# Splitting more of the input projections into upper and lower parts, and moving GpSimd's long steps behind the state space's preparation

## What is computed

```python
z = x @ w_in[i]
u_pool, q, k, v, u_ssm = jnp.split(z, splits, axis=-1)      # 256, 384, 384, 384, 384 columns
y_pool = pool_mixer(u_pool, w_pool[i], pool_scale[i])       # trailing means over 2, 4, 8, 16 tokens
y_attn = chunk_attention(q, k, v, rel_bias[i])              # chunks of 64, own and 8 before
y_ssm = s5_mixer(u_ssm, ...)                                # complex diagonal state space, scan over tokens
heads = jnp.concatenate([rms_norm(y_pool), rms_norm(y_attn), rms_norm(y_ssm)], axis=-1)
h = layer_norm(DN_ALPHA * x + heads @ w_out[i])
x = layer_norm(DN_ALPHA * h + moe(h) + sigmoid(h @ w_ple_gate[i]) * (p[i] @ w_ple_proj[i]))
```

## Time and profile before

| | |
|---|---|
| median of 3 runs | 456.39 us (455.49 to 456.59) |
| the profiled execution's own time | 456.71 us |
| its span | 454.9 us |
| busy: PE, DVE, ACT, POOL | 97%, 74%, 49%, 26% |
| mean granted TensorE clock | 0.993 |

### The profile page before, as it was taken

How to read it: one execution, slowest core, us unless ns; L and a number is a source line. 1 busy time by engine, 2 the same in 40 slices (tenths; PEclk the granted TensorE clock), 3 DMA queues, 4 the chain that set the end, 5 groups by cost and what they waited for, 6 DMA issues and landing times.

```text
span 454.9 us, 5417 instructions
## 1 busy us (share of the span) xinstructions
PE 439.2 (97%) x1933; PEld 297.3 (65%) x1933; DVE 335.7 (74%) x515; ACT 223.5 (49%) x367; POOL 116.2 (26%) x146
## 2 busy tenths in 40 slices
PE   8999999999999999999999999999999999999992
PEld 4444664487676556677687767777777777777651
DVE  3699969885536989998484165778878776789677
ACT  3110461051987850215101155788887777789522
POOL 7880042470056500000007410122212222111200
PEclk9999999999999999999999999999999999999997
DMA  8995023235992981111930239999999999840583
GB/s 273 382 377 161 0 41 87 46 99 152 409 385 72 316 305 46 48 46 55 398 149 2 34 108 424 406 423 418 415 394 369 365 368 371 328 204 20 210 224 139
DMA packets 37049, 103.15 MB, mean 227 GB/s; under 512 B 16028, under 2 KB 22092, under 8 KB 30240
## 3 DMA queue, kind: packets, MB, share of 16 engines
q1 hardware_dynamic: 27728, 91.68, 53.2%
q0 software_dynamic: 5600, 9.44, 6.6%
q10 hardware_dynamic: 3696, 1.71, 1.4%
HBM read 95.39 MB, written 17.86 MB: 249 GB/s over the span
## 4 chain that ended last, share of the span: by engine, by line
PE 70%; DVE 12%; DMA 11%; ACT 4%; issue 1%; SPq 1%; DVEq 0%
PE bank L1298 8%; PE bank L1114 6%; PE bank L946 6%; PE bank L1125 5%; PE bank L1270 5%; DMA region_b<-in_w_exp_down 4%; PE bank L1275 4%; PE bank L1279 4%; PE bank L1283 4%; PE bank L1197 3%; PE bank L1199 3%; PE bank L1198 3%; PE bank L1211 3%; DMA region_b<-in_ssm_par 3%; PE bank L1254 2%; DMA region_b<-expert_scratch 2%
## 5 line engine op out<-in xcount | busy, mean ns | idle before, releaser
L946 PE MATMUL bank<-region_e,region_a 128*128 128x512 f32 x128 | 56.0, 596 | 0.0
L946 PEld LDWEIGHTS bank<-region_e,region_a 128*128 128x128 f32 x128 | 24.0, 190 | 29.7 <-issue 28.7
L1275 PE MATMUL bank<-gate_up_upper,tokens_upper 128*128 128x512 f32 x96 | 36.3, 459 | 0.0
L1114 PE MATMUL bank<-region_b,region_e 128*128 128x512 f32 x68 | 32.9, 607 | 0.0
L568 POOL DMA_INDIRECT slot_scratch<-region_h,slot_i x8 | 8.4, 1054 | 87.2 <-issue 87.2
L581 POOL DMA_INDIRECT expert_scratch<-region_g,region_h x8 | 10.0, 1256 | 80.0 <-ACT region_g L892 80.0
L1823 DVE TENSOR_TENSOR gate_up_lower<-region_a,gate_up_upper 128x1024 fp32r<-128x1024 f32 x24 | 28.0, 1221 | 3.3 <-ACT gate_up_upper L865 3.3
L1279 PE MATMUL bank<-gate_up_upper,tokens_lower 128*128 128x512 f32 x96 | 29.8, 392 | 0.0
L1197 PE MATMUL bank<-ple_gate_upper,hidden_upper 128*128 128x512 f32 x64 | 26.6, 415 | 0.0
L865 ACT ACTIVATE gate_up_upper<-region_a 128x1024 fp32r<-128x1024 f32 x24 | 23.7, 1056 | 3.2 <-DMA region_a<-in_w_exp_down 3.2
L1199 PE MATMUL bank<-ple_gate_upper,hidden_lower 128*128 128x512 f32 x64 | 25.0, 391 | 0.0
(11 more groups left out here) (346 smaller groups left out, 1073.1 us busy)
## 6 DMA issues: line engine op xcount, KB each, us to landing
region_a<-in_w_exp_gate SPq DMA_DIRECT2D x8, 1024.0 KB, 8.1
region_a<-in_w_exp_up SPq DMA_DIRECT2D x8, 1024.0 KB, 17.9
region_a<-in_w_exp_down SPq DMA_DIRECT2D x8, 1024.0 KB, 17.7
region_a<-in_w_in SPq DMA_DIRECT2D x3, 1536.0 KB, 16.6
region_b<-in_w_out SPq DMA_DIRECT2D x1, 4096.0 KB, 14.6
expert_scratch<-zero_scratch SPq DMA_DIRECT2D x8, 512.0 KB, 10.1
region_b<-in_w_exp_gate SPq DMA_DIRECT2D x4, 1024.0 KB, 10.1
region_b<-in_w_exp_up SPq DMA_DIRECT2D x4, 1024.0 KB, 17.6
```

The lines of the kernel that those rows point to most:

```text
L946: last = mm(bank[bank_i][:], w[:, k, m * P:(m + 1) * P], xT[:, k, :], start=(k == 0), stop=(k == KD - 1))
L1114: last = mm(bank[WO_AT[half][group]][:], hdT[:, k, t * P:(t + 1) * P], w_o[:, k, half * 512:half * 512 + 512], start=(i == 0), stop=(i == ...
L1275: mm(out_, x_hi[r][:, k * P:(k + 1) * P], w_hi[:, k], start=False, stop=False)
```

## The change

Six of the eight slices of the state input, all three query tiles and the first key tile are multiplied in upper and lower parts. ACT makes the upper parts (`ux_hi`, `uw_hi` in three pairs of slices, `qw_hi`, `kw_hi`), DVE the lower ones (`u_lower(0..2)`, `qw_lo`, `kw_lo`), into areas that other tensors use later. The loads come in five pairs instead of four, `w_q` stands ahead of `par`. All three query tiles now stand ahead of the first scores, the first pool tile behind the turns, and the last key tile ahead of the second scores. POOL zeroes `m0` after the first key tile (`pe_qk` 4), since `ux_hi` uses its space, and does the doublings of m = 8, 16 and 32 once `cp` and the kernel's inputs are ready (`kern_in` 4). The zero copy of SP waits for that zeroing. DVE normalises heads 0 and 1 behind the scan instead of ahead of the rotation.

```diff
-FIRST_K = (0, 1, 2, 4, KD)
-QK_ORDER = (("q", 0), ("k", 0), ("q", 1), ("q", 2), ("k", 1), ("k", 2))
+FIRST_K = (0, 1, 2, 4, 6, KD)
+QK_ORDER = (("q", 0), ("q", 1), ("q", 2), ("k", 0), ("k", 1), ("k", 2))
@@ sync
+            load(w_q, w_in_v[:, :, POOL_W:POOL_W + ATT_W], "wq_in")
             load(par[:, C_BRE:SSM_COLS], io["ssm_par"][:, C_BRE:SSM_COLS], "par_in")
-            load(w_q, w_in_v[:, :, POOL_W:POOL_W + ATT_W], "wqk_in")
...
-            sp.wait_ge(S["const_set"], 1)
+            sp.wait_ge(S["rot_ready"], 2)
             sp.dma_start(zero_d, RH[:, 3072:3072 + D]).then_inc(S["ye_zero"], 16)
@@ gpsimd
-            link(g.memset(m0, 0.0))
...
             while m < NC:
+                if m == 8:
+                    gp.wait_ge(S["rb_in"], 16)
+                    g.memset(rbias[0:64, :, 192:256], NEG).then_inc(S["rot_ready"], 1)
+                    gp.wait_ge(S["pe_qk"], 4)
+                    g.memset(m0, 0.0).then_inc(S["rot_ready"], 1)
+                    gp.wait_ge(S["kern_in"], 4)
@@ scalar, behind the sines
+            for i in range(3):
+                ac.wait_ge(S[f"x_in{2 + i}"], 32)
+                k = slice(2 + 2 * i, 4 + 2 * i)
+                a.activation(ux_hi[...], xT[:, k, :], ACT.Copy).then_inc(S["xw_hi_set"], 1)
+                a.activation(uw_hi[...], w_ssm[:, k, :], ACT.Copy).then_inc(S["xw_hi_set"], 1)
+            ac.wait_ge(S["wq_in"], 16)
+            a.activation(qw_hi[...], w_q[:, 2:KD, :], ACT.Copy).then_inc(S["xw_hi_set"], 1)
@@ scalar, behind the copies of the state tiles
+            ac.wait_ge(S["wqk_in"], 16)
+            a.activation(kw_hi[...], w_k[:, 2:KD, 0:P], ACT.Copy).then_inc(S["xw_hi_set"], 1)
@@ tensor
+            def u_term(i, w, x, stop=False):
+                for m in range(3):
+                    for k in (2 * i, 2 * i + 1):
+                        last = mm(bank[m][:], w[:, k * SSM_W + m * P:...], x[:, k * T:(k + 1) * T],
+                                  start=False, stop=(stop and k == 5))
+            for i in range(3):
+                pe.wait_ge(S["xw_hi_set"], 2 * i + 2)
+                u_term(i, uw_hi, ux_hi)
+                pe.wait_ge(S["xw_lo_set"], 2 * i + 1)
+                u_term(i, uw_hi, ux_lo)
+                pe.wait_ge(S["xw_lo_set"], 2 * i + 2)
+                u_term(i, uw_lo, ux_hi, i == 2)
+            def qk_split(n, w, w_hi, w_lo, width, parts):
...
+                pe.wait_ge(S["xw_hi_set"], parts)
+                for x in (ux_hi, ux_lo):
...
+                pe.wait_ge(S["xw_lo_set"], parts)
...
-            qk(0)
-            qk(1)
-            project(POOL_BANKS[0], w_up, 0, "pe_pool")
+            for n in range(3):
+                qk_split(n, w_q, qw_hi, qw_lo, ATT_W, 7)
+            pe.wait_ge(S["wqk_in"], 16)
+            qk_split(3, w_k, kw_hi, kw_lo, P, 8)
...
-            pe.wait_ge(S["qk_done"], 2)
+            pe.wait_ge(S["qk_done"], 4)
             scores(0)
@@ vector
+            def u_lower(i):
+                dv.wait_ge(S["xw_hi_set"], 2 * i + 1)
+                tt(ux_lo[...], xT[:, k, :], ux_hi[...], ALU.subtract).then_inc(S["xw_lo_set"], 1)
+                dv.wait_ge(S["xw_hi_set"], 2 * i + 2)
+                tt(uw_lo[...], w_ssm[:, k, :], uw_hi[...], ALU.subtract).then_inc(S["xw_lo_set"], 1)
...
             cmul(bb[:, 0], bb[:, 1], b_re, b_im, ...)
+            dv.wait_ge(S["xw_hi_set"], 7)
+            tt(qw_lo[...], w_q[:, 2:KD, :], qw_hi[...], ALU.subtract).then_inc(S["xw_lo_set"], 1)
...
-            normalise(0)
-            normalise(1)
             dv.wait_ge(S["pe_x"], 1)
-            dv.wait_ge(S["rot_ready"], 1)
+            dv.wait_ge(S["rot_ready"], 3)
...
+            normalise(0)
+            normalise(1)
             add_bias(2)
```

More of the change, by code:

```diff
@@ L246, in trunk @@
         hd_lo = {k: over(f"heads_lower{k}", T - P, R0 + 4 * (k * T + P)) for k in WO_SPLIT}
+        ux_hi = over("input_upper", 6 * T, H0 + 4 * 3072)
+        uw_hi = over("state_weights_upper", 6 * SSM_W, C0)
+        ux_lo = over("input_lower", 6 * T, C0 + 4 * 3072)
+        qw_hi = over("query_weights_upper", 6 * ATT_W, G0 + 4 * 1536)
+        qw_lo = over("query_weights_lower", 6 * ATT_W, A0 + 4 * (O_Q + 2 * ATT_W))
+        kw_hi = over("key_weights_upper", 6 * P, H0 + 4 * 6144)
+        kw_lo = over("key_weights_lower", 6 * ATT_W, A0 + 4 * (O_K + 2 * ATT_W))
+        uw_lo = over("state_weights_lower", 6 * SSM_W, A0 + 4 * 2 * SSM_W)
         bank = [ctx.enter_context(nc.psum_tensor(f"bank{i}", [P, 512], F32)) for i in range(8)]
@@ L320, in _ @@
             xv = io["xT"].rearrange("(p k) t -> p k t", k=KD)
-            for i in range(4):
+            for i in range(5):
                 ks = slice(FIRST_K[i], FIRST_K[i + 1])
@@ L508, in _ @@
             link(g.tensor_copy(dec, mag8[:].unsqueeze(2).broadcast_to([P, Q, NC])))
[L509 to L512, removed]
+            g.memset(dec[:, :, 0:1], 0.0).then_inc(S["rot_ready"], 1)
+            gp.wait_ge(S["rot_ready"], 3)
             gp.wait_ge(S["gp_in"], 16 * 4)
@@ L683, in _ @@
             qk_copy(1)
+            qk_copy(2)
             ac.wait_ge(S["bx_ready"], 2)
@@ L951, in _ @@
                 mm(bank[7][:, 0:P], ones[:], ones[:], start=True, stop=True)
-            for k in range(KD):
-                if k in FIRST_K:
-                    pe.wait_ge(S[f"x_in{FIRST_K.index(k)}"], 32)
+            for k in range(2):
+                pe.wait_ge(S[f"x_in{k}"], 32)
                 for m in range(3):
-                    last = mm(bank[m][:], w_ssm[:, k, m * P:(m + 1) * P], xT[:, k, :], start=(k == 0), stop=(k == KD - 1))
-                    if k == KD - 1:
-                        last.then_inc(S["pe_u"], 1)
+                    mm(bank[m][:], w_ssm[:, k, m * P:(m + 1) * P], xT[:, k, :], start=(k == 0), stop=False)
+            def u_term(i, w, x, stop=False):
+                for m in range(3):
+                    for k in (2 * i, 2 * i + 1):
+                        last = mm(bank[m][:], w[:, k * SSM_W + m * P:k * SSM_W + (m + 1) * P], x[:, k * T:(k + 1) * T],
+                                  start=False, stop=(stop and k == 5))
+                    if stop:
+                        last.then_inc(S["pe_u"], 1)
+            for i in range(3):
[5 more added lines that the diff above has]
+                u_term(i, uw_lo, ux_hi, i == 2)
             def qk(n):
@@ L962, in qk @@
                 project(QK_BANKS[n], w_q if name == "q" else w_k, m, "pe_qk")
+            def qk_split(n, w, w_hi, w_lo, width, parts):
+                _, m = QK_ORDER[n]
+                dst = bank[QK_BANKS[n]][:]
+                for k in range(2):
+                    mm(dst, w[:, k, m * P:(m + 1) * P], xT[:, k, :], start=(k == 0), stop=False)
+                pe.wait_ge(S["xw_hi_set"], parts)
+                for x in (ux_hi, ux_lo):
+                    for k in range(6):
+                        mm(dst, w_hi[:, k * width + m * P:k * width + (m + 1) * P], x[:, k * T:(k + 1) * T], start=False, stop=False)
+                pe.wait_ge(S["xw_lo_set"], parts)
+                for k in range(6):
+                    last = mm(dst, w_lo[:, k * ATT_W + m * P:k * ATT_W + (m + 1) * P], ux_hi[:, k * T:(k + 1) * T], start=False, stop=(k == 5))
+                last.then_inc(S["pe_qk"], 1)
             def v_tile(t, bank_i):
```

53 lines of the change are left out of this document (35 added, 18 removed).

## The result

The changed kernel takes 466.76 us in the median of 6 runs (465.59 to 467.53), the kernel before 456.14 (455.35 to 456.59): the ratio is 1.023 [1.021, 1.025]. It is slower by 2.3%, outside the range of the prediction, whose forecast was 0.2% faster. The profiled execution took 465.68 us, 9.0 more than that of before.

What follows compares the result with a forecast made beforehand. TensorE was taken as full, VectorE as almost as long, with Y held by the moved states. Y starting 0.9 us earlier gave 456.7 - 0.9 = 455.8, on the runs' scale 455.5 us; range 453.7 to 458.3.

Steps and rivals of the forecast that it cites:

- What bounds the kernel, and that the moved states decide Y's start: TensorE full, VectorE almost as long; the moved states release the Y stage at 93.6 instead of 94.5, 0.9 us earlier.
- TensorE's saving: 42 split matmuls take 7.8 us off TensorE, which stands at Y at 89.5, 5.0 us earlier than before.
- The idle time at the third slice: TensorE waits for ScalarE's rounding after slices 0 and 1: 2.4 us idle until 12.8, against 0.45 before.
- ssm_par 4.1 us later, 22.2: Load queued behind the query weights; VectorE's complex product starts at 22.2, 4.1 us later.
- The lower parts, the steps without GpSimd beside them: VectorE: lower parts add 2.6 and 1.0 us, steps without GpSimd give near 6.9 back; cp ends at 56.9.
- The zeroing beside cp costs nothing: GpSimd's zeroing of m0 at 49 to 52 beside VectorE's 3072-column products: 0 taken, bounds 0 and 2.7 us.
- GpSimd's 13.0 us now on the path: GpSimd's late doublings and decay copy behind cp take 13.0 us and release the rotation at 70.0.
- The wait ahead of Y: TensorE, ready early, waits about 4 us ahead of the Y stage for the moved states.
- The fall in it: Clock falls from 2.4 to 1.2 GHz some 2.2 us after TensorE stops, read from the kernel's end.
- The forecast's own sum: Profiled time 456.7 less 0.9 us for Y's earlier start gives 455.8, or 455.5 on the runs' scale.
- the first rival: Clock falls in the wait ahead of Y, costing 1.6 to 1.8 us of Y: 457.2; chance 0.26.
- The bound from the row: Upper bound of the clock rival's loss: 10.8 us if all of Y ran at half rate.

Runs made afterwards that it cites:

- the fill: Changed kernel plus five thrown-away 384-column matmuls on TensorE ahead of its wait for the Y stage: 455.03 us, ratio 0.997.
- the doubling: Changed kernel with GpSimd's last doubling (32 columns a group) moved to VectorE: four executions at 452.8 to 454.6 us, two at 461.8 and 462.1.
- both: Changed kernel with the last doubling on VectorE and two thrown-away matmuls ahead of the wait for Y: 453.13 us, ratio 0.994.
- the fourth term: Changed kernel with a lower-by-lower term added to each of its 42 split products: 461.88 us, ratio 1.012.
- three additions: Kernel before plus three thrown-away VectorE additions of 1536 columns ahead of the last step of the scanned states: 474.18 us, ratio 1.039.
- two additions: Kernel before plus two thrown-away VectorE additions of 1536 columns ahead of the last step of the scanned states: 470.99 us, ratio 1.031.
- dense work behind the wait: Changed kernel plus eight thrown-away 384-column matmuls on TensorE behind the wait, ahead of Y: 460.15 us, ratio 1.008.
- long steps early: Changed kernel with GpSimd's doublings of 8, 16 and 32 run at once again, m0's zeroing and a memset behind them: 460.24 us, ratio 1.009.
- one addition: Kernel before plus one thrown-away VectorE addition of 1536 columns ahead of the last step of the scanned states: 457.32 us, ratio 1.003.

## Why the prediction was wrong

Point by point:

- *What bounds the kernel, and that the moved states decide Y's start*: right. Y was released by the moves in the changed kernel, and the start came 2.05 us earlier, of which 0.9 had been forecast.
- *TensorE's saving* (89.5 at Y): right, 89.4. The idle time at the third slice was 0.65 us in this profile, since slices 0 and 1 took 6.3 us instead of 5.42 (an instruction there took up to 1.22 us against 0.59, so TensorE was still at half rate) and ScalarE began to round the third at 10.0 instead of 10.8; it was 2.2 to 2.5 in the runs with the fill, the doubling, both, and the fourth term; Y's side did not need it.
- *ssm_par 4.1 us later, 22.2*: VectorE began bb at 21.64. *The lower parts, the steps without GpSimd beside them*: 0.23 and 0.24 us where 0.20 and 0.25 were taken, 2.56 for the query weights' where 2.6 was. cp ended 1.0 us earlier than said.
- *The zeroing beside cp costs nothing*: right, 3.36 us. By the Trainium skill's rule ("SBUF — State Buffer", who interferes with whom), an instruction of GpSimd that only writes does not block one of VectorE with two SBUF inputs; the trace agrees.
- *GpSimd's 13.0 us now on the path*: 13.1, and the rotation was released by GpSimd.
- *The wait ahead of Y*: 3.1 us where about 4 were said. *The fall in it* came 2.7 us after TensorE had stopped, where the rival had 2.2 from the kernel's end.

The step that failed is the price of the clock. The forecast's own sum, 456.7 - 0.9, has no term for it: it was left to the first rival, and priced there as "Half rate for as long costs 1.6 to 1.8 us of Y (bounds: 0, and 10.8 if all of Y ran so)". The mechanism and its place had been named, with a chance of 0.26; its size was not 1.7 but 9.9 us in Y and 1.4 in the scores, the upper bound and more. I had carried the time that the clock needed to rise from the kernel's start, where the matmuls of 128 columns on ones stand back to back, to Y, where 96 instructions of 64 columns each load new weights (PEld is busy 2.00 of 2 us). Under those it did not rise: 20.7 us at half rate in the changed kernel and in the one with three additions, 17.8 in the one with two. Under other work it did: 6.1 us into the fills (dense work behind the wait), 2.6 to 3.1 us into the scores in four profiles, and 5.0 us behind Y in that of the doubling on VectorE. Even the start was read too short: in the profile of the changed kernel slices 0 and 1 lost 0.88 us, which by an estimate is twice that, 1.8 us, at half rate beyond the 3.7 taken. The bound from the row was there and was left out of the range. The rival made the kernel slower only "if the loss passes 2.3 us", a third of its cases; the measured loss passes that in each of the six executions.

The chance was off as well. Sorted by the wait ahead of Y in the profiled execution:

| kernel | wait, us | executions in which the clock fell for Y |
|---|---|---|
| before; changed and filled; long steps early; fourth term; doubling and fill | 0 to 0.1 | none seen |
| before, one addition | 0.30 | 0 of 10 |
| doubling on VectorE | 0.69 | 2 of 6 |
| changed | 3.08 | 6 of 6 |
| before, two additions | 3.76 | 4 of 4 |
| before, three additions | 5.25 | 5 of 5 |

(Counted by total time and mean clock: 0.965 to 0.974 where it fell, 0.989 and more where it did not; 0.985 and 0.986 with the long steps early, whose fall was ahead of the first scores.) The changed kernel lies on the sure side in each of its executions, not at one in four.

So the account of the change is: 2.05 us won at Y's start, 9.9 lost in Y, 1.4 in the scores, together 9.2 in the profiled execution, where spans differ by 8.5. The medians differ by 10.6. The 1.6 us between are not accounted for; the six executions of the changed kernel spread over 1.9.

Why a wait of 0.69 us is enough in two executions of six, and why the fall can come after Y has begun, was not settled. Counted from where TensorE stopped, the clock fell after 2.3 to 2.7 us in the profiles of the changed kernel, of the fills behind the wait and of the long steps early, but after 3.4 with the doubling on VectorE, 4.6 with three additions and 5.3 with two. No run varied Y's own matmuls, so what it is in them that does not bring the clock back (their 64 columns, their weight loads, the number of them) is not shown. Whether the useful work of a value tile could take the place of the fill was not tried.

The Trainium skill ("TensorE: Matmul & The Clock Gate", on the clock gate) says that the throttled state is the default and activity releases it. The runs agree in part: the clock falls behind an idle stretch, and came back under the fills and under the scores; but Y, busy throughout, stayed at half rate to its end.

## What to carry to other kernels

When a change takes work from TensorE ahead of a stage of short matmuls with a weight load each, ask first whether the stage's other inputs come earlier too: a wait that opens ahead of such a stage can cost not its own length but nearly the whole stage a second time (here 9.9 us on 10.8; the clock fell in every execution of the kernels that waited 3.1 us or more directly ahead of it). Price a fall of the clock by the length of the stage behind it, not by the time that the clock took to rise elsewhere, and look at PEclk, since busy columns do not show it. Where such a wait can't be closed from the other side (here, by giving VectorE's idle time the last of GpSimd's three late doublings), filling it with matmuls that nobody reads can be worth several times their time (11.7 us for 3.3 here).

## What the runs showed of the hardware

- A wait of TensorE does not cost the clock by its length alone. Before the third slice it waited 2.2 us in the run with doubling and fill, and matmuls of 512 columns followed; the clock stayed at 1.00. The doubling alone, the fill and the fourth term show the same, with 2.35 to 2.52 us:

```profile
12.00:13.00 1.00, 0.52 (x2) 0.48 (x3) 0.93 (x3) 0.42 (x1) 0.76 (x4) 1.00 1.04 391
```

- Full matmuls of 64 columns at 0.22 us each with their weight loads kept the full clock for 10.8 us where they were entered without a wait (before, and with the fill), yet did not regain it in 20.7.
- VectorE's bias additions, with an operand in PSUM, and its row maxima were not slowed by GpSimd's doublings beside them (from 55.84 on they took 6.9 us, and 6.9 before, when GpSimd was idle). The third normalisation, at 97.8, took 5.0 us beside GpSimd's pooling, and the fourth 1.27 alone.
